# Attention weights of six heads turned by VectorE and a trip through DRAM instead of TensorE

## What is computed

```python
z = jnp.einsum('bhtd,bhsd->bhts', qb, kb).astype(jnp.float32) * scale
log_beta = jax.nn.log_sigmoid(z)
log_skip_j = jnp.where(causal, jax.nn.log_sigmoid(-z), 0.0)
log_skip = lax.cumsum(log_skip_j, axis=3, reverse=True) - log_skip_j
weights = jnp.where(causal, jnp.exp(log_beta + log_skip), 0.0)
outs.append(jnp.einsum('bhts,bhsd->bhtd', weights.astype(vb.dtype), vb))
```

## Time and profile before

| | us |
|---|---|
| median of three runs | 1175.18 |
| span of the profiled execution | 1173.5 |
| PE busy | 1163.8 |
| DVE busy | 796.7 |
| ACT busy | 419.7 |
| POOL busy | 149.8 |

### The profile page before, as it was taken

One profiled execution on the slowest core, in us unless ns is written; L12 is line 12 of the kernel. 1 busy time (PEld: TensorE's weight loads), 2 busy tenths in 40 slices (PEclk: granted clock), 3 DMA queues, 4 the chain that ended last, 5 costly groups with the idle time before them and its releaser, 6 DMA issues. The chain is left out here.

```text
span 1173.5 us, 20148 instructions
## 1 busy us (share of the span) xinstructions
PE 1163.8 (99%) x7228; PEld 1071.4 (91%) x7228; DVE 796.7 (68%) x1612; ACT 419.7 (36%) x911; POOL 149.8 (13%) x344
## 2 busy tenths in 40 slices
PE   8999999999999999999999999999999999999998
PEld 8999999999999999888888989898999999999787
DVE  5757485766767675774444778788888888788421
ACT  5535353545445454452222222323232322222200
POOL 2422121203031211110003100000000000000000
PEclk9999999999999999999999999999999999999999
DMA  8210223223142301066632110314142421117441
GB/s 251 57 53 19 73 82 112 68 83 103 67 119 73 109 1 46 1 228 218 209 108 73 55 36 20 115 66 137 70 145 72 133 86 45 45 37 296 148 139 72
DMA packets 110659, 113.51 MB, mean 97 GB/s; under 512 B 6880, under 2 KB 86752, under 8 KB 110560
## 3 DMA queue, kind: packets, MB, share of 16 engines
q1 hardware_dynamic: 110560, 112.23, 30.1%
HBM read 79.70 MB, written 32.51 MB: 96 GB/s over the span
## 5 line engine op out<-in xcount | busy, mean ns | idle before, releaser
L28 PE MATMUL p_proj<-w_qkv_hi,ut_hi 128*128 128x384 f32 x504 | 172.0, 341 | 0.2 <-DVE ut_lo L796 0.2
L30 PE MATMUL p_proj<-w_qkv_hi,ut_lo 128*128 128x384 f32 x504 | 169.1, 336 | 0.0
L29 PE MATMUL p_proj<-w_qkv_lo,ut_hi 128*128 128x384 f32 x504 | 168.7, 335 | 0.0
L28 PE MATMUL p_proj<-w_ig_hi,next_hi 128*128 128x256 f32 x512 | 145.5, 284 | 0.0
L29 PE MATMUL p_proj<-w_ig_lo,next_hi 128*128 128x256 f32 x512 | 143.1, 279 | 0.0
L30 PE MATMUL p_proj<-w_ig_hi,next_lo 128*128 128x256 f32 x512 | 143.0, 279 | 0.0
L28 PE MATMUL p_proj<-next_hi,w_qf_hi 128*128 128x512 f32 x282 | 113.2, 402 | 0.0
L30 PE MATMUL p_proj<-next_hi,w_qf_lo 128*128 128x512 f32 x282 | 110.1, 390 | 0.0
L29 PE MATMUL p_proj<-next_lo,w_qf_hi 128*128 128x512 f32 x282 | 109.8, 390 | 0.0
L808 DVE TENSOR_TENSOR_SCAN a_skip<-a_skip,a_diagonal 128x129 f32<-128x129 f32 (+3 forms) x64 | 86.9, 1358 | 30.2 <-ACT a_beta L648 28.4
L28 PEld LDWEIGHTS p_proj<-w_ig_hi,next_hi 128*128 128x128 f32 x512 | 96.2, 188 | 0.0
(11 more groups left out here) (255 smaller groups left out, 2732.3 us busy)
## 6 DMA issues: line engine op xcount, KB each, us to landing
stage<-in_hg_w_in_dram SPq DMA_DIRECT2D x32, 512.0 KB, 4.3
stage<-in_sb_w_in_dram SPq DMA_DIRECT2D x29, 512.0 KB, 5.9
w_out_hi_scratch<-m_in SPq DMA_DIRECT2D x32, 256.0 KB, 2.1
w_out_lo_scratch<-m_in SPq DMA_DIRECT2D x32, 256.0 KB, 2.3
m_in<-mixed_scratch SPq DMA_DIRECT2D x12, 448.0 KB, 6.1
a_beta<-in_x_dram SPq DMA_DIRECT2D x8, 512.0 KB, 4.3
m_in<-in_sb_w_out_dram SPq DMA_DIRECT2D x16, 256.0 KB, 3.6
ut_hi<-w_out_hi_scratch SPq DMA_DIRECT2D x8, 512.0 KB, 8.7
```

The costliest lines, as they stand in the source:

```text
L28: pe.matmul(out, w_hi, m_hi, start=start, stop=False, skip_group_check=True)
L29: pe.matmul(out, w_hi, m_lo, start=False, stop=False, skip_group_check=True)
L30: return pe.matmul(out, w_lo, m_hi, start=False, stop=stop, skip_group_check=True)
```

## The change

For heads 0 to 5 (`CARRIED`) PE no longer turns the weights. After `weigh(i)` DVE transposes them in blocks of 32x32 into the skip buffer (`flip`), SP stores this to DRAM, waits for it, and loads it back with four DMAs of 32 partitions each into the tile's beta buffer, so that the blocks stand turned (`carry`). Beta has three buffers for these heads. ACT and DVE round the landed weights two uses after the scores (`settle`, in a new part "mid" of the plan), now from SBUF. The value products move one use later, into the middle of a projection; the last pair of a head goes into use 0 of the next step. `sigmoids(i)` waits for the store of tile i-2 and for the low part of tile i-3. The high and low parts have a new layout in which a tile's 128 queries stand in four groups of 32. Heads 6 and 7 are turned by PE as before, into the new layout.

To make room, `squares` has one buffer, the scaled k is written into `raw`, and the input tiles share the gate buffers. The halves of the output matrix are split at the ends of uses 1, 2, 4 and 5 and their DMAs stand between the carries; the loads into `stage` are issued by ACT at the ends of uses 5 and 9. The row semaphores are shared by both layers, with a count per layer.

```diff
-             "after": {i: ([("outputs", 0, (i - 3) // 2)] if i >= 3 and i % 2 == 1 else []) +
-                       ([("turn", 0, i - 1)] if 1 <= i <= TILES else []) for i in range(USES)}}
+             "mid": {i: ([("outputs", 0, i // 2 - 2)] if i >= 4 and i % 2 == 0 else []) +
+                        ([("settle", 0, i - 2)] if i >= 2 else [("outputs", -1, PAIRS - 1)] if i == 0 else [])
+                     for i in range(USES)},
+             "after": {}}
...
-    SPLIT_AT = [5, 6, 7, 9]
+    SPLIT_AT = [1, 2, 4, 5]
+    OUTPUTS_AT = KT // 2
+    SPLITS_AFTER = {1: ("store", 0), 2: ("load", 2), 3: ("store", 1), 4: ("load", 3), 5: ("store", 2), 6: ("store", 3)}
...
-        squares = [sb(f"squares{i}", [P, P]) for i in range(2)]
+        squares = sb("squares", [P, P])
-        k_scaled = [sb(f"k_scaled{i}", [P, P]) for i in range(4)]
-        beta = [sb(f"beta{i}", [P, SEQ]) for i in range(2)]
+        beta = [sb(f"beta{i}", [P, (7 * P, SEQ, 6 * P)[i]]) for i in range(3)]
-        wt_hi = sb("wt_hi", [P, TILES, 2, P], F32R)
+        wt_hi = sb("wt_hi", [P, 2, 4, TILES, QUARTER], F32R)
...
+        def flipped_blocks(h, i):
+
+            run = (i + 1) * QUARTER
+            return weights_of(h, i)[:, 0:4 * run].rearrange("p (g r) -> p g r", g=4)
...
+            def carry(h, j, group):
+
+                sp.wait_ge(flipped, TILES * h + j + 1)
+                run = (j + 1) * QUARTER
+                sp.dma_start(flips[j, :, 0:4 * run], skip[j % 2][:, 0:4 * run]).then_inc(flip_stored[j % 2], 16)
+                sp.wait_ge(flip_stored[j % 2], 16 * (PAIRS * h + j // 2 + 1))
+                for c in range(4):
+                    if c == 1 and group is not None:
+                        for i in range(2):
+                            sp.wait_ge(link["w_parts_stored"][i], group * 64 + 64)
+                    sp.dma_start(flipped_blocks(h, j)[c * QUARTER:(c + 1) * QUARTER, :, :],
+                                 flips[j, :, c * run:(c + 1) * run].rearrange("(g p) r -> p g r", g=4)
+                                 ).then_inc(carried[j % 3], 16)
+
+            def carry_all(h, b, group, previous=None):
+
+                if group is not None:
+                    for i in range(2):
+                        load_raw_half(sp, m_in, w_out, link, group, i)
+                for j in range(TILES):
+                    carry(h, j, group if j == TILES - 1 else None)
+                    if j == 0 and previous is not None:
+                        store(previous, 1 - b)
+                    if group is not None and j in SPLITS_AFTER:
+                        what, part = SPLITS_AFTER[j]
+                        if what == "load":
+                            load_raw_half(sp, m_in, w_out, link, group, part)
+                        else:
+                            store_half(sp, m_in, w_out, link, group, part)
...
-                        if i >= 2:
-                            act.wait_ge(weights_turned, UNITS * h + ENDS[i - 2])
+                        if is_carried(h) or h == CARRIED and i < 2:
+                            if i >= 2 or not known_first(h):
+                                act.wait_ge(flip_stored[i % 2], 16 * (PAIRS * h + i // 2))
+                            if not is_carried(h):
+                                act.wait_ge(wt_ready, UNITS * (h - 1) + ENDS[6 + i])
+                            elif i >= 3:
+                                act.wait_ge(wt_ready, UNITS * h + ENDS[i - 3])
...
+            def settle_weights(h, j):
+
+                act.wait_ge(carried[j % 3], 64 * ((3, 3, 2)[j % 3] * h + j // 3 + 1))
+                if j >= 2 or not known_first(h):
+                    act.wait_ge(o_done, PAIRS * h + j // 2)
+                act.activation(slot_of(wt_hi, j), flipped_blocks(h, j), ACT.Copy).then_inc(wt_hi_ready, Z_UNITS[j])
...
+                    if plan is PLAIN and i == 5:
+                        load(h + 2, 3)
+                    if plan is PLAIN and i == USES - 1 and not (isinstance(h, int) and h == HEADS - 3):
+                        for p in range(3):
+                            load(h + 3, p)
...
+            def flip(h, i):
+
+                width = (i + 1) * P
+                dve.wait_ge(weights_ready, TILES * h + i + 1)
+                dve.transpose(skip[i % 2][:, 0:width].rearrange("p (c s i) -> p s c i", c=4, i=QUARTER),
+                              weights_of(h, i)[:, 0:width].rearrange("p (s c i) -> p s c i", c=4, i=QUARTER)
+                              ).then_inc(flipped, 1)
...
                     if what == "scores":
                         weigh(head, tile)
+                        if plan is PLAIN:
+                            flip(head, tile)
+                    elif what == "settle":
+                        refine_weights(head, tile)
...
+            def refine_weights(h, j):
+
+                dve.wait_ge(wt_hi_ready, UNITS * h + ENDS[j])
+                dve.tensor_tensor(slot_of(wt_lo, j), flipped_blocks(h, j), slot_of(wt_hi, j).bitcast(F32),
+                                  ALU.subtract).then_inc(wt_ready, Z_UNITS[j])
...
                 for s in range(2 * g + 2):
-                    w_h = wt_hi[:, s, :, :] if s <= 2 * g else wt_hi[:, s, 1, :]
+                    tiles = slice(0, 2) if s <= 2 * g else 1
+                    w_h = wt_hi[:, tiles, :, s, :]
...
+                            if kt == OUTPUTS_AT:
+                                attend(h, b, plan, "mid", i)
```

More of the change, by code:

```diff
@@ L63, in build_trunk, with link @@
         m_in = [sb(f"m_in{i}", [P, HEADS, P]) for i in range(2)]
-        def link(tag):
+        row_loaded = [ctx.enter_context(nc.semaphore(f"row_loaded{r}")) for r in range(HEADS)]
+        def link(tag, layer):
             def sem(name):
@@ L73, in link @@
                     "rows_free": sem("rows_free"),
-                    "row_loaded": [sem(f"row_loaded{r}") for r in range(HEADS)],
+                    "row_loaded": row_loaded,
+                    "row_landed": 32 * (layer + 1),
                     "stored": sem("mixed_stored"),
@@ L440, in build_attention @@
         weights_ready = sem("weights_ready")
+        flipped = sem("flipped")
+        flip_stored = [sem(f"flip_stored{i}") for i in range(2)]
+        carried = [sem(f"carried{i}") for i in range(3)]
         weights_turned = sem("weights_turned")
@@ L464, in of_head, with of_plan @@
             return (h, b) if d == 0 else (h + d, 1 - b)
+        def of_plan(plan, when, h, i):
+            return [entry for entry in plan[when].get(i, []) if entry[1] >= 0 or not known_first(h)]
         def turn_events(plan, projects, first_head):
@@ L469, in turn_events @@
             for i in range(USES):
-                for when in ("before", "after"):
+                for when in ("before", "mid", "after"):
                     if when == "after" and projects and i >= 3 and i % 2 == 1:
@@ L570, in _ @@
                              allow_slow_non_contiguous=True).then_inc(small_loaded, 16)
[L571 to L575, removed]
+            carry_all(0, 0, None)
             with sp.Fori(0, 2) as pair:
                 for b in (1, 0):
[L578 to L581, removed]
+                    carry_all(pair * 2 + 2 - b, b, pair * 2 + 1 - b, pair * 2 + 1 - b)
+            carry_all(HEADS - 3, 1, None, HEADS - 4)
             store(HEADS - 3, 1)
@@ L603, in split_hi, with load @@
                 act.activation(dst, stage[p][:, :, :], ACT.Copy).then_inc(w_hi_ready[p], 1)
+            def load(h, p):
+                act.wait_ge(w_ready[p], h)
+                load_columns(act, stage, w_in, h, p).then_inc(w_loaded[p], 16)
             def split_hi_half(p, u):
@@ L647, in sigmoids @@
                                    scale=inv_rms[b][i][:, 2:3])
-                    act.activation(beta[i % 2][:, cols], p_z[unit % 3][:, 0:width], ACT.Sigmoid,
+                    act.activation(weights_of(h, i)[:, cols], p_z[unit % 3][:, 0:width], ACT.Sigmoid,
                                    scale=inv_rms[b][i][:, 0:1]).then_inc(sigmoids_ready, 1)
             def attend(h, b, plan, when, i):
-                for what, d, tile in plan[when].get(i, []):
+                for what, d, tile in of_plan(plan, when, h, i):
                     head, half = of_head(h, b, d)
@@ L660, in attend @@
                             copy_weights(head, tile, u, turn_bank(plan, event))
+                    elif what == "settle":
+                        settle_weights(head, tile)
                     elif what == "mixed":
@@ L732, in step @@
                             split_hi(n + 1, p)
+                    if plan is FIRST and i == USES - 1:
+                        for p in range(3):
+                            load(2, p)
                     if plan is SQUEEZED and i == USES - 1:
@@ L810, in weigh @@
                 dve.wait_ge(scan_done, TILES * h + i + 1)
-                dve.tensor_tensor(beta[i % 2][:, 0:width], beta[i % 2][:, 0:width],
+                weights = weights_of(h, i)[:, 0:width]
```

(7 more changed lines are left out.)

77 lines of the change are left out of this document (50 added, 27 removed).

## The result

The changed kernel takes 1207.8 us (median of four runs, 1207.1 to 1209.2) where the kernel before takes 1175.2: the ratio is 1.028, with a 95% interval of 1.026 to 1.029. It is 32.6 us slower. The forecast was 1175.9 with a range up to 1189.

The account below looks back on a forecast made before the run. PE, busy 1163.8 of 1173.5 us and waiting for almost nothing, was taken as the bound. The sum was 1175.2 - 23.8 for the turns + 24.5 for waits = 1175.9 us, range 1160 to 1189.

Parts of the forecast that it names:

- The turns: 216 weight turns leave PE in heads 0 to 5, at 0.11 us each: 23.8 us won.
- The strided value products: PE's 360 passes in heads 0 to 5, reading 32-element runs 1 KB apart: no cost, bounds 0 and 4 us.
- The chain: ACT and DVE alternate from use 4 to tile 5's low part: 30.5 us against PE's 27.0, so 3.5 us wait per head.
- the low parts with those of q and k: DVE's low parts of tiles 2 to 5, 2.7 us, and of q and k in uses 5 and 7, 1.5 us.
- Rivals A: Rounding is ready in time at the value products, so all 23.8 us are won: 1151 or 1156 us; chance 0.12.
- C: DVE's strided flips run at half rate between ACT's sigmoids: 4.1 us more per head, 1200 us; chance 0.04.
- D: Tile 5's loads land after ACT wants them in use 7: 3 us more per head, 1194 us; chance 0.04.
- The w_out half: ACT's split of the fourth half, ending use 5, delays tile 6's sigmoids in heads 1 to 4: +0.5 us each, bounds 0 and +2.
- rival B: TensorE's clock falls in waits of 4 us, slowing following work: 2 us in each of six heads, 1188 us; chance 0.08.
- small things: Unlisted items, such as the wait in `squares` and slower SBUF under more traffic: 1.5 us added in all.
- Its own sign of being wrong: The prediction is wrong if PE's waits add up to under 15 or over 35 us.
- the second value products: Wanted by PE 3.3 us into use 6, with their low part ready at about 2.9 us: just in time.

Follow-up runs that it names:

- the kernel without waits: Against the changed kernel: flip after the low part, fourth w_out half split at use 6, value products before a projection's last step; 1152.7 us, ratio 0.981.

## Why the prediction was wrong, by its own steps

**The turns: right.** 23.8 us forecast, 22.8 measured in the kernel without waits. The strided value products, taken at nothing with 4 us as a bound, cost some 0.1 us a head.

**The chain: right mechanism, 0.6 us a head short.** Forecast was that sigmoids(i) waits for the low part of tile i-3, that the flips stand in between, and that PE waits 3.5 us at the third products. In heads 0 and 5, which have no w_out half, it waited 4.1 us, with ACT's sigmoids released by line 954. Of head 5 the trace gives 31.2 us from the scores of use 4 to the end of the low part of tile 5, where the sum had 30.5; PE's own path took 27.2, where it had 27.0. Start, sigmoids, scans and flips came out as listed (1.5, 8.4, 11.8 and 4.2). Short were the low parts with those of q and k, 4.65 us from the ends of the flips for 2.7 + 1.5, and the hand-overs, about 0.7 for 0.3. A term was missing: in uses 5 and 7 `gate_outputs` (line 970, the row at 315.99 above) stands on DVE between the flip and the low part and moves it by 0.3 us each time.

Rivals A (the chain isn't the bound), C (flips at half rate) and D (landings late) are out: A by the waits, C by flips of 1.25 us for 1024 columns and 1.11 for 896. Of D, the trip was indeed longer than the 7 us estimated in places: from the store's issue to the last landing it took 4.6 to 10.5 us. But ACT's only wait of over 0.4 us for a landed tile in the changed kernel is 0.8 us in head 3, right ahead of the 6.65 us for the w_out half, and heads 0 and 5 have none.

**The w_out half: the step that failed first, by its size.** "I take +0.5, with 0 and +2 as bounds." Heads 1 to 4 waited 2.8 to 3.1 us more than heads 0 and 5 at the products, and up to 1.4 more at the scores. With the half one use later PE's waits fell from 39.6 to 25.0 us, so the term was worth 14.6 us in all, where the prediction had 4 x 0.5 = 2. SP's queue in uses 4 to 6 of head 3 shows why:

```profile
291.83 0.36 SPq L271 DMA_DIRECT2D m_in<-in_sb_w_out_dram  x1
292.31 0.36 SPq L582 DMA_DIRECT2D flips_scratch<-a_skip  x1
296.79 2.20 SPq L588 DMA_DIRECT2D a_beta<-flips_scratch  x4
299.16 0.36 SPq L295 DMA_DIRECT2D w_out_hi_scratch<-m_in  x1
299.62 0.37 SPq L295 DMA_DIRECT2D w_out_lo_scratch<-m_in  x1
300.11 0.38 SPq L582 DMA_DIRECT2D flips_scratch<-a_skip  x1
303.37 1.75 SPq L588 DMA_DIRECT2D a_beta<-flips_scratch  x4
305.31 0.36 SPq L271 DMA_DIRECT2D m_in<-in_sb_w_out_dram  x1
```

I let the store of tile 4 start as soon as the flip was done (296.95). SP was then still in the carry of tile 3: its store, issued at 292.31 right behind a load of w_out, landed only 4.5 us later, and four loads and two w_out stores came next, so that the store of tile 4 left at 300.11, 3.2 us late. It landed after 3.2 us where 2.4 were taken, and the load of the half after 3.7 where 3 to 3.6 were. That load landed 13.1 us into use 5 (308.99, with the scores at 295.90) where the sum had 8.5. The queue was walked for its order but not for its times: each carry holds SP from the issue of its store to the landing, and the next one starts when the one before it ends, flip or no flip.

**The clock: left out of the sum, the second step that failed.** It was named as rival B, at 12 us and a chance of 0.08. It fell in all six heads, and the price was about right: PE was busy for 26 us of the 41 at half clock, so about 13 us were lost, an estimate that counts half of the busy time; 10.6 us are the measured difference of the two runs with and without turns in the waits. For the low chance the prediction gave no reason. It noted that no wait of before was over 1.6 us and that no row shows at which length the clock drops, which says nothing of the waits of 4 us that it had just forecast. The page of the Trainium skill that I named beside it, "TensorE: Matmul & The Clock Gate", Part 1, states that idling brings the array to half rate, and here the trace agrees: granted clock 0.51 to 0.54 in the windows around the waits. The forecast should have been the chain's wait plus the fall of the clock that follows from it, one case and not two.

**The sum.** In terms of the profiled spans: -22.8 for the turns, +39.6 for the waits, about +1.7 because the idle time of a wait is counted from the end of the pass before it: that pass takes 0.39 us in the rows above, and without a wait the next one starts 0.22 to 0.23 us after it, so each of the ten waits costs some 0.17 us more than is shown, +13 to 14 for the clock. This gives +31.5 to 32.5; measured +32.8, and what makes up the rest is open. The prediction had -23.8, +24.5 and no clock term. Of the 15.1 us that its waits were short, the w_out half is 12.6 and the chain 4.0, less the 1.5 that it had added for small things. Its own sign of being wrong, waits of over 35 us in all, was met. The clock alone, added to its 1175.9, would not have reached the measured time either.

**What the prediction had nearly right and drew no use from.** It said that the second value products were just in time (3.3 us into use 6, ready at 2.9). In head 3 they begin at 304.98, and the low part of tile 3 ended at 304.93: the chain had no time left already there, and each step of it that was under-sized went straight into PE's wait.

## What to carry to other kernels

Where buffers rotate between two engines, look whether the release of a buffer sits on the consumer's queue behind the next tile's work: here ACT's sigmoids waited for a low part that DVE did only after the next scan and flip, and changing the order of two DVE instructions was worth 24 us. Once a wait is forecast on TensorE, its clock belongs to the same case. When a transfer is queued behind others on a queue that also waits for landings, add up that queue's times from the first entry, as for any other engine, and ask for each moved consumer who stands behind it.

## What the runs showed of the hardware

After waits of PE of 3.5 us and more, the granted clock went to half in every case in these runs; after waits of up to 1.8 us it never did. Of three between 2.1 and 2.4 us, the two that stood behind thirty turns were without a fall, and the one in the kernel with the flip last alone had one. The fall began between 2.0 and 5.3 us after PE had stopped: in head 3 of the changed kernel 4.7 us before PE went on, in head 0 only after it (PE goes on at 115.8 and the clock falls at 116.6). In either case work that follows pays for it. Where a wait was filled with turns of the identity so that 1.1 us at most were left, the clock stayed up (mean 1.000); at the start of the run before, turns with nothing else on PE go from 421 ns to 280 and then 272.

DVE's transpose of 128x1024 took 1.245 us in the four-dimensional form, the same as in the flat form of the earlier trace rows, and 0.31 us for 128 columns, with 0.133 us for each 128 columns more. Four loads of 32 partitions each, 128 KB, landed in 2.9 us at the median; the stores of the flipped tiles (128 to 512 KB) took 2.4 to 4.7, as medians of each size, single ones 1.8 to 5.7.
